# The triangular solve of a gated delta layer: its first doubling moved into the gates stage, blocks up to 16 in 32-wide tiles, one mask by ScalarE

## The reference, cut to what matters

```
G = jnp.cumsum(gc, axis=-1)
decay = jnp.where(causal, jnp.exp(jnp.where(causal, diff, 0.0)), 0.0)   # diff = G_i - G_j
kk = jnp.einsum("bhnid,bhnjd->bhnij", k_beta, kc)
lower = jnp.eye(c, dtype=f32) + jnp.where(strict, kk * decay, 0.0)
uw = lax.linalg.triangular_solve(lower, rhs, left_side=True, lower=True)
attn = jnp.einsum("bhnid,bhnjd->bhnij", qc, kc) * decay
```

## Time and profile before

| | |
|---|---|
| median of 3 runs | 2184.0 us (2180.01 to 2184.84) |
| the profiled execution | 2180.5 us, its span 2178.6 us |
| gates, solve of layer 0 | 221.8 to 242.2 us, 242.2 to 286.1 us |
| gates, solve of layer 1 | 602.5 to 622.8 us, 622.8 to 663.0 us |
| mean granted TensorE clock | 0.979 of 2.4 GHz |

### The profile page before, as it was taken

The page is one execution under the profiler, slowest core; times in us unless marked ns, Lnnn a source line. Parts: engine busy times, 40 slices in busy tenths (PEclk is TensorE's granted clock), DMA queues, the critical chain, the costliest instruction groups (busy, mean ns, idle before and its releaser), DMA issues. The chain is left out here.

```text
span 2178.6 us, 28146 instructions
## 1 busy us (share of the span) xinstructions
PE 2049.3 (94%) x11508; PEld 1617.5 (74%) x11508; DVE 1172.6 (54%) x1452; ACT 858.9 (39%) x1237; POOL 340.2 (16%) x310
## 2 busy tenths in 40 slices
PE   8999889899988989988999999999998999999996
PEld 4677886577787668644778888877888877888885
DVE  4545637554564753243478447645333857745753
ACT  4246424524543351355344234332122724423431
POOL 0200615120062520143220000012000012000003
PEclk9999989999999999999999999999999989999998
DMA  5211103221111222200222232233221022223221
GB/s 222 75 61 39 41 6 112 97 78 58 39 41 42 75 97 94 95 16 1 80 94 91 87 103 97 86 117 116 97 96 40 2 72 67 88 93 116 97 80 65
DMA packets 30402, 167.46 MB, mean 77 GB/s; under 512 B 2795, under 2 KB 9379, under 8 KB 14660
## 3 DMA queue, kind: packets, MB, share of 16 engines
q1 hardware_dynamic: 30276, 165.69, 22.0%
HBM read 159.35 MB, written 10.00 MB: 78 GB/s over the span
## 5 line engine op out<-in xcount | busy, mean ns | idle before, releaser
L281 PE MATMUL psum<-inputs_high,weights_high 128*128 128x512 f32 x928 | 382.9, 413 | 25.9 <-DVE inputs_low L248 16.6
L282 PE MATMUL psum<-inputs_low,weights_high 128*128 128x512 f32 x928 | 367.4, 396 | 0.0
L283 PE MATMUL psum<-inputs_high,weights_low 128*128 128x512 f32 x928 | 367.3, 396 | 0.0
L2009 PE MATMUL psum<-inputs_high,weights_high 128*128 128x512 f32 x704 | 276.3, 392 | 4.9 <-DVE inputs_low L2145 4.9
L2010 PE MATMUL psum<-inputs_low,weights_high 128*128 128x512 f32 x704 | 274.3, 390 | 0.0
L2011 PE MATMUL psum<-inputs_high,weights_low 128*128 128x512 f32 x704 | 274.3, 390 | 0.0
L253 DVE TENSOR_TENSOR weights_low<-weights_raw,weights_high 128x2048 fp32r<-128x2048 f32 x69 | 162.0, 2348 | 178.0 <-ACT weights_high L242 178.0
L281 PEld LDWEIGHTS psum<-inputs_high,weights_high 128*128 128x128 f32 x928 | 176.0, 190 | 83.3 <-DVE inputs_low L248 20.8
L242 ACT CAST weights_high<-weights_raw 128x2048 fp32r<-128x2048 f32 x69 | 130.9, 1898 | 193.5 <-PE psum L283 178.0
L282 PEld LDWEIGHTS psum<-inputs_low,weights_high 128*128 128x128 f32 x928 | 176.2, 190 | 40.9 <-issue 5.0
L283 PEld LDWEIGHTS psum<-inputs_high,weights_low 128*128 128x128 f32 x928 | 176.1, 190 | 39.9
(11 more groups left out here) (357 smaller groups left out, 3275.1 us busy)
## 6 DMA issues: line engine op xcount, KB each, us to landing
weights_raw<-w_stream SPq DMA_DIRECT2D x116, 1024.0 KB, 4.8
weights_raw<-w_down SPq DMA_DIRECT2D x32, 704.0 KB, 4.0
residual_parked<-residual SPq DMA_DIRECT2D x2, 2048.0 KB, 11.2
residual_back<-residual_parked SPq DMA_DIRECT2D x2, 2048.0 KB, 7.8
residual<-x_t SPq DMA_DIRECT2D x1, 2048.0 KB, 7.7
bias_by_row<-bias_rows SPq DMA_DIRECT2D x2, 1024.0 KB
out_t<-residual SPq DMA_DIRECT2D x8, 256.0 KB, 2.0
bias_by_row<-bias_rows SPq DMA_DIRECT2D x1, 1536.0 KB
```

The source lines that it names most:

```text
L281: pe.matmul(out, hi, self.ahi[:, k], start=start and b == 0, stop=False)
L282: pe.matmul(out, hi, self.alo[:, k], start=False, stop=False)
L283: mm = pe.matmul(out, lo, self.ahi[:, k], start=False, stop=stop and b == blocks - 1)
L2009: pe.matmul(out, wh, hi, start=start, stop=False)
```

## The change

- Gates: VectorE forms the four chunks' differences of a head in one instruction, GpSimd fills with a large negative number before the exponential, not with zero after it, and the k-by-k reads wait for the exponentials. GpSimd multiplies the coupling of all four chunks by the negated mask of level 0. After each q-by-k pair TensorE does `left(t)`: identity and coupling accumulate in PSUM, two matmuls for each corner; ScalarE copies the corners to x, and VectorE adds the identity to ct for xt. GpSimd then prepares the level-1 masks of two chunks. `a.qg` and `a.elast` move to the end of GpSimd's stream in the solve.
- Solve: it starts at level 1. Levels 1 to 4 use the four diagonal 32 x 32 tiles of each head in place of the two 64 x 64 corners. The mask of level 4 is made by ScalarE (a copy of the upper columns, scaled by a 0/1 column) after GpSimd has cleared the lower ones.
- x moves to `k.raw[:, 1]`. The first weight chunk is issued when `a.qg` and `a.elast` are done, the second when the last `left` is done.

```diff
+NEVER = -1.0e4
...
+    h[:, H_ROWS] = np.arange(P) % 32 < 16
+    h[:, H_FIRST:H_FIRST + P] = -level_mask(LEVELS[0])
...
-                        act.wait_ge(s.diff, 4 * n)
+                        act.wait_ge(s.masked, n)
...
+                act.wait_ge(s.kb, HEADS)
+                act.activation(ps[:, 2:4].rearrange("p b i -> p (b i)"), k.hcon[:, 0:2 * T], ACT.Copy, scale=0.0) \
+                    .then_inc(s.zero_both, 1)
+                act.wait_ge(s.pair, TT)
+                for t in range(TT):
+                    act.wait_ge(s.left, t + 1)
+                    for r in square_tiles(P // 2):
+                        act.copy(x[r, t, :, r], bank(4 + t % 2)[r, :, r]).then_inc(s.inv, 1)
...
-                    for t in range(TT):
-                        dve.tensor_scalar(decay[:, t, n], row[:, t], gcol[:, t, n:n + 1], 0.0,
-                                          ALU.subtract, ALU.min).then_inc(s.diff, 1)
+                    column = gcol[:, :, n:n + 1].to_broadcast([P, TT, P])
+                    dve.tensor_tensor(decay[:, :, n], row, column, ALU.subtract).then_inc(s.diff, 1)
...
+                def first(t):
+                    identity = ident.unsqueeze(1).to_broadcast([P, HEADS, P])
+                    dve.wait_ge(s.coupled, t + 1)
+                    dve.wait_ge(s.pair_read, TT + t + 1)
+                    dve.tensor_tensor(xt[:, t], identity, ct[:, t], ALU.add).then_inc(s.inv_t, 1)
+                dve.wait_ge(s.decay, HEADS)
+                for t in range(TT):
+                    pair(t)
+                for t in range(TT):
+                    pair(TT + t)
+                    first(t)
...
-                    pool.wait_ge(s.decay, n + 1)
-                    pool.affine_select(out=decay[:, :, n], in_=decay[:, :, n], compare_op=ALU.is_ge, fill=0.0, base=0,
+                    pool.wait_ge(s.diff, n + 1)
+                    pool.affine_select(out=decay[:, :, n], in_=decay[:, :, n], compare_op=ALU.is_ge, fill=NEVER, base=0,
                                        pattern=[[0, TT], [1, P]], channel_multiplier=-1).then_inc(s.masked, 1)
-                for n in range(HEADS):
-                    pool.wait_ge(s.row_exp, n + 1)
-                    pool.tensor_tensor(a.qg[:, n], q[:, n], erow[:, n], ALU.mult).then_inc(s.scaled, 1)
-                    pool.tensor_copy(a.elast[:, n], erow[:, n].rearrange("p (t i) -> p t i", t=TT)[:, :, P - 1]) \
-                        .then_inc(s.scaled, 1)
-
+                masks = [m.unsqueeze(1).to_broadcast([P, HEADS, P])
+                         for m in (k.hcon[:, H_FIRST:H_FIRST + P], level_mask_of(k.hcon, 1))]
                 pool.wait_ge(s.turned, HEADS)
-                mask = level_mask_of(k.hcon, 0).unsqueeze(1).to_broadcast([P, HEADS, P])
+                for t in range(TT):
+                    pool.wait_ge(s.pair_read, t + 1)
+                    pool.tensor_tensor(ct[:, t], a.at[:, t], masks[0], ALU.mult).then_inc(s.coupled, 1)
                 for t in range(COUPLED):
-                    pool.wait_ge(s.pair_read, t + 1)
-                    pool.tensor_tensor(coupling[:, t], a.at[:, t], mask, ALU.mult).then_inc(s.coupled, 1)
+                    pool.wait_ge(s.left, t + 1)
+                    pool.wait_ge(s.inv_t, t + 1)
+                    pool.tensor_tensor(ct[:, t], a.at[:, t], masks[1], ALU.mult).then_inc(s.coupled, 1)
...
+                def left(t):
+                    pe.wait_ge(s.coupled, t + 1)
+                    if t >= 2:
+                        pe.wait_ge(s.inv, 2 * t - 2)
+                    for hd in range(HEADS):
+                        for r in square_tiles(P // 2):
+                            out, one = bank(4 + t % 2)[r, hd, r], ident[r, r]
+                            pe.matmul(out, one, one, start=True, stop=False)
+                            mm = pe.matmul(out, ct[r, t, hd, r], one, start=False, stop=True)
+                    mm.then_inc(s.left, 1)
+                for n in range(TT):
+                    pair(n)
                     if n in (1, 3):
                         turn(HEADS + 2 + n // 2)
+                for t in range(TT):
+                    pair(TT + t)
+                    left(t)
...
+def solve_homes(k, h):
+    cx, ct = [h.qkv[:, 4 * n:4 * n + 4].rearrange("p t (h i) -> p t h i", h=HEADS) for n in (1, 2)]
+    return k.raw[:, 1].rearrange("p (t h i) -> p t h i", t=TT, h=HEADS), cx, ct
+def square_tiles(size):
+    return [slice(size * r, size * r + size) for r in range(P // size)]
...
-                for u in range(2):
-                    sp.dma_start(k.raw[:, u], k.w_stream[layer * HYBRID_CHUNKS + PROJ_CHUNKS + u]).then_inc(k.landed[u], 16)
+                sp.wait_ge(s.row_used, 2 * HEADS)
+                sp.dma_start(k.raw[:, 0], k.w_stream[layer * HYBRID_CHUNKS + PROJ_CHUNKS]).then_inc(k.landed[0], 16)
+                sp.wait_ge(s.left, steps)
+                sp.dma_start(k.raw[:, 1], k.w_stream[layer * HYBRID_CHUNKS + PROJ_CHUNKS + 1]).then_inc(k.landed[1], 16)
...
-                        for r in corners():
-                            mm = pe.matmul(left_bank(t)[r, hd, r], ct[r, t, hd, r], x[r, t, hd, r] if n else ident[r, r],
+                        for r in tiles(n):
+                            mm = pe.matmul(left_bank(t)[r, hd, r], ct[r, t, hd, r], x[r, t, hd, r],
...
-                        for r in corners():
+                        for r in tiles(n):
                             pe.matmul(both_bank(t, 0)[r, hd, r], xt[r, t, hd, r], cx[r, t, hd, r], start=True, stop=True)
-                        for r in corners():
+                        for r in tiles(n):
                             mm = pe.matmul(both_bank(t, 1)[r, hd, r], cx[r, t, hd, r], xt[r, t, hd, r],
                                            start=True, stop=True)
...
-                pe.wait_ge(s.zero_left, 1)
-                for t in range(TT):
-                    left(0, t)
-                for m in range(first_step, steps + behind):
+                for m in range(steps + behind):
                     if m < steps:
-                        left(m // TT, m % TT)
-                    if m - behind >= first_step:
-                        both((m - behind) // TT, (m - behind) % TT)
+                        left(m // TT + 1, m % TT)
+                    if m >= behind:
+                        both((m - behind) // TT + 1, (m - behind) % TT)
...
+                    if n == by_rows - 1:
+                        act.activation(upper(ct[:, t], by_rows), upper(a.at[:, t], by_rows), ACT.Copy,
+                                       scale=k.hcon[:, H_ROWS:H_ROWS + 1]).then_inc(s.rows_kept, 1)
...
+                for n in range(1, by_rows):
                     mask = level_mask_of(k.hcon, n).unsqueeze(1).to_broadcast([P, HEADS, P])
-                    for t in range(0 if n else COUPLED, TT):
-                        if n:
-                            pool.wait_ge(s.left, 4 * (n - 1) + t + 1)
-                            pool.wait_ge(s.inv_t, t + 1)
+                    for t in range(COUPLED if n == 1 else 0, TT):
+                        if n > 1:
+                            pool.wait_ge(s.left, place(n, t) - TT + 1)
                         pool.tensor_tensor(ct[:, t], a.at[:, t], mask, ALU.mult).then_inc(s.coupling, 1)
+                for t in range(TT):
+                    pool.wait_ge(s.left, place(by_rows, t) - TT + 1)
+                    pool.memset(lower(ct[:, t], by_rows), 0.0).then_inc(s.cleared, 1)
+                for n in range(HEADS):
+                    pool.tensor_tensor(a.qg[:, n], q[:, n], erow[:, n], ALU.mult).then_inc(s.row_used, 1)
+                    pool.tensor_copy(a.elast[:, n], erow[:, n].rearrange("p (t i) -> p t i", t=TT)[:, :, P - 1]) \
+                        .then_inc(s.row_used, 1)
```

More of the change, by code:

```diff
@@ L84 @@
 H_RESET = H_LEVEL + 2 * P * len(LEVELS)
-N_HYBRID = H_RESET + T
+H_ROWS = H_RESET + T
+H_FIRST = H_ROWS + 1
+N_HYBRID = H_FIRST + P
 def level_mask(s):
@@ L877, in delta_gates @@
             nc, "row", "row_exp", "diff", "row_read", "decay", "masked", "kb", "scaled", "turned", "turned_read",
-            "last_arg", "last_exp", "pair", "pair_read", "coupled") as s:
+            "last_arg", "last_exp", "pair", "pair_read", "coupled", "left", "inv", "inv_t", "zero_both") as s:
         def sb(name, shape):
@@ L928, in _, with pair @@
                     dve.tensor_tensor(a.kbg[:, n], kb[:, n], erow[:, n], ALU.mult).then_inc(s.scaled, 1)
-                for n in range(2 * TT):
+                def pair(n):
                     t = n % TT
                     dve.wait_ge(s.pair, n + 1)
-                    dve.wait_ge(s.masked, HEADS)
                     dst = a.at if n < TT else a.attn
@@ L1008, in solve @@
     mid = last - 1
+    by_rows = mid - 1
     half, quarter = P // 2, P // 4
-    first_step, steps, behind = TT, TT * n_levels, 2
+    steps, behind = TT * last, 2
+    q, erow = h.qkv[:, 0:4], k.raw[:, 0].rearrange("p (h i) -> p h i", h=HEADS)
```

(20 more changed lines are left out.)

45 lines of the change are left out of this document (20 added, 25 removed).

## The result

The changed kernel takes 2216.3 us (median of 4 runs, 2213.9 to 2219.6) against 2184.4 (4 runs) in the same measurement, a ratio of 1.0161 with the interval 1.0149 to 1.0173. It is slower, and 2220 was forecast. The profiled execution is the slowest of the four, 2219.55 us with a span of 2217.9; that of the kernel before took 2180.5. So the traces lie 39 us apart and the medians 32.

The account below looks back on a forecast made before the run. TensorE's instruction supply, one packet of 253 per 3.9 us, was taken to bound the solve. Gates 2 x 4.0, solves 55.9 each (before 43.9 and 40.1) and transfers 3 gave +38.8 us: 2220 us forecast, range 2196 to 2242.

Parts of the forecast that it names:

- The supply of instructions (theory A): TensorE's instruction fetch: about 253 instructions per packet, one packet per 3.9 us (3.85 in the experiments), paces the solve.
- a whole number of packets lies between two halts: Kernel before, between the two layers' halts: 5265 instructions, 20.8 packets of 253, read as halts at packet borders.
- The solve: Levels 1 to 6 of each layer: 0.4 + 1.3 + 50.7 + 3.5 = 55.9 us, before 43.9 and 40.1.
- one packet in store: At the solve's start one packet is running and the next loaded; each further one stored would save 3.9 us a solve.
- The gates: Each layer's gates: -0.35 + 3.7 + 0.5 + 0.1 = +4.0 us, bounds +3.4 and +7.9.
- the term of 0.5 us for eight changes: TensorE's tail of the gates: 0.5 us for eight changes of tile size around the four added lefts.
- The transfers: Weight transfers crossing instruction fetches in the solve: a late packet costs 1.5 us a layer, bounds 0 and 4.
- The sum: Whole kernel: 2 x 4.0 + (55.9 - 43.9) + (55.9 - 40.1) + 3 = +38.8 us on the profiled 2180.5.
- Fetches keep up: Rival: in the solves packets come sooner when requested sooner; solves of 28.8 and 26.1 us, 2160 us; chance 0.10.
- Packets of 3.0 us under demand: Rival: in the solves fetches come faster under steady demand but still bind; 23 us less, 2196 us; chance 0.08.
- Narrow records as dear as wide ones: Rival: in levels 1 to 4 each narrow record costs 29.2 ns, a step 2.8 us; +35, 2215 us; chance 0.03.
- The clock: TensorE's clock may stay at 0.50 through the solve; no cost beside packets, up to 3 us in layer 1's scans.

Follow-up runs that it names:

- -4 packets: The changed kernel with the lefts of levels 1 to 4 in 64-wide corners and only the reads into x and xt in 32-wide tiles: 2204.3 us.
- +4 packets: The changed kernel with eight further 32-wide identity matmuls at each left of levels 1 to 4, into a bank nobody reads: 2231.1 us.
- +12 packets on the kernel before: The kernel before with only its tiles of levels 1 to 4 made 32-wide: 2220.3 us, against 2180.3 for the kernel before on that chip.
- 32-wide with two heads: The changed kernel with heads 2 and 3 left out of levels 1 to 4, all tiles still 32-wide: 2177.6 us.
- late transfers: The changed kernel with the first weight chunk issued after the solve's last left: 2215.8 us; repeated 2219.1 us, beside 2219.9 for the changed kernel.

## Why the prediction was right

**The supply of instructions (theory A).** Four changes of the count move the time by it: -12 packets with wide corners 38 us, -4 packets 12 us, +4 packets 11 to 15 us (against the two medians of the changed kernel), and +12 packets on the kernel before 40 us. That is 3 to 4 us for each. Kernels of equal count but different tile size (64-wide; 32-wide with two heads) take 35.8 and 35.7 us against 36.4 and 36.0 for the solves. The trace of the changed kernel also shows the parts of a packet's interval. From 250 to 260 us, in slices of 0.25 us, the packets are these:

```profile
GB/s 66 0 0 0 0 0 0 0 0 0 0 0 0 0 66 0 0 0 0 0 0 0 0 0 0 0 0 0 0 66 0 0 0 0 0 0 0 0 0 0
```

They start at about 250.2, 253.6 and 257.4 us, and the halts shown above end at 252.49, 256.17 and 259.85. So TensorE goes on 2.3 to 2.5 us after a packet's start, and the next packet starts only 1.1 to 1.2 us after TensorE has gone on; together that is the interval. The kernel before has the same at its halt, with 64-wide tiles; this is its DMA from 270 to 282 us, in slices of 0.3 us:

```profile
GB/s 0 0 0 0 0 0 0 0 0 55 0 0 0 0 0 0 0 0 0 0 0 0 55 0 0 0 0 0 0 0 0 0 0 0 55 0 0 0 0 0
```

A packet starts at about 276.7, TensorE goes on at 279.04, and the next packet starts at about 280.3. So at each of these halts one packet is under way at a time, and the next waits until it is in use; more demand doesn't bring them closer. What takes the time within either part isn't shown. The reading in the prediction that a whole number of packets lies between two halts is weak: 5,265 records are 20.9 to 20.7 packets of 252 to 254, and TensorE's waits before have no "issue" in layer 1. The forecast didn't rest on it.

**The solve.** Forecast: packets from 1.7 us after the gates, 13 of 3.9 us, and 3.5 us behind the last: 1.7 + 50.7 + 3.5 = 55.9. Measured in layer 0: 13 packets as counted, the first about 2.8 us after the gates' end, twelve intervals of 3.8 (46 us), and 7.7 from the last one's start to the end (forecast as 3.9 + 3.5 = 7.4): 56.3. Layer 1 has 58.9, its intervals being 4.0 to 4.1. With the 1.5 us for transfers the forecast was 57.4 for each, and the mean of the two is 57.6. The assumption of one packet in store was right (TensorE ran 396 records from the start of the solve to its first halt, one and a half packets); the first is fetched 1 us later than I had it, and the intervals of layer 0 are 0.1 us shorter.

**The gates.** +4.0 forecast, +4.6 measured in both layers. This is the timeline of their tail, TensorE then ScalarE:

```profile
237.74 1.06 PE L1024 MATMUL psum<-qkv 128*128 128x128 f32 x8
238.72 0.34 PE L1036 MATMUL psum<-constants 64*64 64x64 f32 x4
...
239.59 0.33 PE L1037 MATMUL psum<-constants,qkv 64*64 64x64 f32 x4
239.85 1.16 PE L1024 MATMUL psum<-qkv 128*128 128x128 f32 x8
```
```profile
246.60 0.76 ACT L932 COPY weights_raw<-psum 64x256 f32<-64x256 f32 x2 [1.46 <-PE psum L1037]
```

The q-by-k pairs start 14.05 us after the gates do (before 14.44): the head gained 0.39, forecast 0.35. From there to the end of the gates it was 4.62 us and is 9.62: 5.0 more, forecast 4.3. The pair's pitch went from 0.97 us (3.89 / 4) to 2.11 and then 2.2. Of the 1.24 us more, 0.94 is the left's own; the other 0.3 stands where TensorE changes to 64-wide tiles and back, which the term of 0.5 us for eight changes had at 0.125. The mis-sized term is this one: 1.2 us measured. GpSimd's masks were ready in time, as forecast.

**The transfers.** The term of 3 us (bounds 0 and 4) isn't borne out. Traces show the late packet, and the solves with late transfers are 0.9 to 4 us shorter; but two comparisons by medians give no difference. So its value is nearer the lower bound, 0. Where a late packet's time goes isn't settled. The trace with late transfers has solves 5.6 us shorter in all than the changed kernel's and a span only 2.5 shorter; 2.0 of the rest lie ahead of the first gates' end, in work that no edit touches and that differs so much from one execution to the next. In part the profiled executions mislead: that of the changed kernel was the slowest of its runs in both measurements (2219.55 of four, 2224.63 of five).

**The sum.** +38.8 forecast against the profiled execution, +39.3 between the spans, closer than the terms deserve, since their errors cancel: each layer's gates 0.6 too small, the solves together, with the transfers' 3 us, 0.4 too small, and outside the two stages 1 us less. By the medians it is 32 to 39 us (2216.3 less 2184.4, 2219.9 less 2181.3).

**The rivals.** *Fetches keep up*: 2160. The halts of 22.7 us refute it for this kernel. Its solves would have been 28.8 and 26.1 us; even wide corners, which hardly outrun the supply, took 33. The rule of the page "Runtime: NRT & Kernel Launch" of the Trainium skill (Instruction fetch mechanics), that fetches stay hidden, fails here too. *Packets of 3.0 us under demand*: none of the mean intervals is under 3.6. *Narrow records as dear as wide ones* (2215, near the truth by chance): the 9 ns a record in the trace and the halts between bursts refute it; the run with two heads doesn't, as said there. A forecast of the time alone wouldn't have told this rival from the right one. *The clock*: it fell to 0.50, 1.2 GHz, at about 254 us, after TensorE's first halt of 1.76 us and as its second began, and the solve's mean is 0.56. The 126 or 127 matmul records between two halts then take 1.95 us in place of 1.36 (the windows above), and the packets come no later for it. Nor does it cost anything visible behind the solve: the first 10 us of the scans have 0.75 and 0.73 after, and 0.62 and 0.83 before.

## What to carry to other kernels

Count TensorE's instructions of a stage, four for each fp32 matmul (two weight loads and two matmul records), and divide by 253: where small matmuls run at more than about 65 of them per us for longer than a packet or two, the supply (one packet per 3.8 to 4.1 us here) sets the pace, and halving the tile while doubling the count makes the stage longer by 3 to 4 us for each packet (here the solve went from 36 to 56 and 59 us). The sign in a trace is idle time for "issue" in the middle of a group, at equal counts of records. Then wider tiles with wasted columns are the faster ones: with the doubling moved to the gates and corners of 64, the same algorithm takes 0.995 of the time instead of 1.016.

## What the runs showed that I had not expected

- A wait that is already satisfied isn't free on TensorE: 18 such instructions took at most about 1.7 us, 0.1 us each, ten times a 32-wide matmul record (9 ns); and 36 waits make 18 instructions.
- A transfer of 1 MB beside the solve delays one packet visibly (intervals of 5.4 and 6.6 us instead of 3 to 4.5) if the packet falls into it, and the kernel's median doesn't show it.
- Work that alternates two tile sizes costs 0.3 us a round trip, and can still be the better order, because it covers another engine's read.
- The steady 64-wide levels, with TensorE busy throughout, were at the edge of the supply already (69 records per us used, 65 brought); nothing but the short halt of the earlier trace rows showed it.
